# One gate tile of each of the first three attention rounds moved into the last round of a hybrid decoder layer

## What is computed

```python
n = rmsnorm(h) ; proj = n @ w_in         # q_A k_A v_A q_B k_B v_B (512 each) gate_A gate_B (1024 each)
o_a = dilated_attention(rope(q_a), rope(k_a), v_a)      # 8 heads of 64
o_b = stick_breaking_attention(q_b, k_b, v_b)           # 8 heads of 64
mixed = sigmoid(gate_a) * (o_a @ w_up_a) + sigmoid(gate_b) * (o_b @ w_up_b)
h = h + mixed @ w_out
h = h + memory_attention(rmsnorm(h), rmsnorm(mem))
h = h + swiglu(rmsnorm(h)) ; return rmsnorm(h)
```

## Time and profile before

| | us |
|---|---|
| median of 3 runs (lowest, highest) | 1866.86 (1864.33, 1867.20) |
| the profiled execution's own time | 1866.63 |
| its span, first to last instruction | 1864.8 |
| PE busy | 1733.5 (93% of the span) |
| DVE busy | 1143.5 (61%) |
| ACT busy | 777.6 (42%) |
| POOL busy | 766.9 (41%) |
| start of the four rounds on PE | 121.09, 299.10, 476.35, 653.69 |
| start of the gated stage on PE | 818.35 |

### The profile page before, as it was taken

The page is one execution under the profiler, slowest core; times in us unless marked ns, Lnnn a source line. Parts: engine busy times, 40 slices in busy tenths (PEclk is TensorE's granted clock), DMA queues, the critical chain, the costliest instruction groups (busy, mean ns, idle before and its releaser), DMA issues.

```text
span 1864.8 us, 24982 instructions
## 1 busy us (share of the span) xinstructions
PE 1733.5 (93%) x8346; PEld 1401.5 (75%) x8346; DVE 1143.5 (61%) x1688; ACT 777.6 (42%) x1283; POOL 766.9 (41%) x892
## 2 busy tenths in 40 slices
PE   3799999999999999969999887999999999999996
PEld 3677777777777777758887765788888888788884
DVE  6446795689468856965444568645545455566666
ACT  4214773577358647852222344433433334110012
POOL 5732222332223221224454112665666656533445
PEclk8899999999999999979999888999999999999998
DMA  5311112111211211164212000122121221332222
GB/s 185 134 40 43 42 50 66 46 29 57 69 36 39 67 51 40 50 245 147 102 45 91 23 12 22 46 104 76 67 90 67 97 83 67 139 108 92 90 90 91
DMA packets 51711, 141.73 MB, mean 76 GB/s; under 512 B 6192, under 2 KB 14640, under 8 KB 51504
## 3 DMA queue, kind: packets, MB, share of 16 engines
q1 hardware_dynamic: 30816, 98.73, 15.0%
q10 hardware_dynamic: 20816, 41.95, 6.8%
HBM read 109.20 MB, written 30.41 MB: 75 GB/s over the span
## 4 chain that ended last, share of the span: by engine, by line
PE 79%; DVE 6%; issue 5%; ACT 3%; POOL 2%; ACTq 0%; DMA 0%; DVEq 0%; POOLq 0%
PE ps L492 45%; PE ps L811 22%; PE ps L638 4%; PE ps L601 3%; PE ps L615 3%; POOL w_lo L461 1%; DVE e_row L1530 1%; POOL rms L473 1%; DVE pt L1560 1%; DVE e_row L1527 1%; DVE h L1889 1%; DVE rows L1539 1%; PE ps L634 1%; POOL w_lo L446 0%; ACT p_m L1173 0%
## 5 line engine op out<-in xcount | busy, mean ns | idle before, releaser
L441 POOL TENSOR_SCALAR w_hi<-w_stage 128x512 fp32r<-128x512 f32 x188 | 128.3, 700 | 884.5 <-issue 457.9
L446 POOL TENSOR_TENSOR w_lo<-w_stage,w_hi 128x256 fp32r<-128x256 f32 x376 | 346.7, 952 | 7.9
L492 PE MATMUL ps<-n_hi,w_hi 128*128 128x512 f32 x1184 | 329.9, 400 | 14.2 <-DVE n_lo L1480 7.1
L492 PE MATMUL ps<-n_lo,w_hi 128*128 128x512 f32 x1184 | 321.8, 393 | 0.0
L492 PE MATMUL ps<-n_hi,w_lo 128*128 128x512 f32 x1184 | 321.2, 392 | 0.0
L492 PEld LDWEIGHTS ps<-n_hi,w_hi 128*128 128x128 f32 x1184 | 222.1, 191 | 62.7 <-issue 16.5
L492 PEld LDWEIGHTS ps<-n_lo,w_hi 128*128 128x128 f32 x1184 | 221.9, 189 | 46.0 <-issue 0.2
L492 PEld LDWEIGHTS ps<-n_hi,w_lo 128*128 128x128 f32 x1184 | 220.2, 188 | 44.9
L461 POOL TENSOR_TENSOR w_lo<-w_stage,w_hi 128x256 fp32r<-128x256 f32 x176 | 163.7, 950 | 146.9 <-ACT w_hi L1207 146.9
L1630 DVE TENSOR_TENSOR h<-ps,h 128x512 f32<-128x512 f32 (+1 forms) x176 | 121.3, 690 | 127.2 <-PE ps L492 127.2
L1029 ACT ACTIVATE pt<-ps 128x256 fp32r<-128x256 f32 (+3 forms) x96 | 78.0, 812 | 134.9 <-PE ps L615 134.9
(11 more groups left out here) (224 smaller groups left out, 2997.2 us busy)
## 6 DMA issues: line engine op xcount, KB each, us to landing
w_stage<-weights_in SPq DMA_DIRECT2D x116, 512.0 KB, 3.4
w_stage<-weights_in SPq DMA_DIRECT2D x44, 256.0 KB, 2.7
hidden_scratch<-u_f SPq DMA_DIRECT2D x22, 512.0 KB, 5.7
n_lo<-hidden_scratch SPq DMA_DIRECT2D x22, 512.0 KB, 4.0
gates_scratch<-raw ACTq DMA_DIRECT2D x16, 512.0 KB, 2.8
o_scratch<-o_sum ACTq DMA_DIRECT2D x64, 64.0 KB, 2.1
n_lo<-o_scratch ACTq DMA_DIRECT2D x8, 512.0 KB, 4.1
g_a<-gates_scratch ACTq DMA_DIRECT2D x8, 512.0 KB, 3.7
```

What stands on the lines that cost most here:

```text
L441: ins = pool.tensor_scalar(w_hi[:, b, at], stage[:, b, at], 1.0, 1.0, ALU.mult, ALU.mult)
L446: ins = pool.tensor_tensor(w_lo[:, b, at], stage[:, b, at], w_hi[:, b, at].bitcast(F32), ALU.subtract)
L492: ins = pe.matmul(bank, w[:, b, c:c + P], mv(k), start=(first and n == 0), stop=(last and n == total - 1))
```

## The change

The first three rounds get three gate tiles instead of four, and the last round seven instead of four, 9, 9, 9 and 10 tiles in place of 10, 10, 10 and 7. In the first three rounds the value tile of B now stands ahead of the query and key tile of A, and one pass is gone from each of slots 0 to 5. The last round has passes in all its 28 slots. The rounds are written out (Python loops in place of `Fori`), so that all semaphore counts and addresses in them are constants. `LOAD_O` and `ROUND_O` are gone: all eight output tiles are loaded, rounded and split behind the last pass of the last round (ACT waits for `bank_full` of `B_GATED`). The total number of passes is the same (222).

```diff
-TILES_IN = 10
+TILES_IN = 9
+GATES_IN = 3
-ROUND = Plan(("KB", "QB", "QA", "KA", "VB", "VA", "G0", "G1", "G2", "G3"),
-             [3] * 6 + [2] * 6 + [3, 2, 3, 2, 3, 2, 2, 3, 2] + [1] * 6 + [2], {"TB": (12, 14), "TA": (18, 20)})
-LAST = Plan(("KB", "QB", "VB", "G0", "G1", "G2", "G3"),
-            [2] * 21 + [0] * 7, {"TB": (10, 12)})
-LOAD_O = {max(LAST.end.values()) + 2 + n: [k for k in (2 * n, 2 * n + 1) if k < KT - 1] for n in range(4)}
-ROUND_O = {min(LOAD_O) + 3 + k: k for k in range(4)}
+ROUND = Plan(("KB", "QB", "VB", "QA", "KA", "VA", "G0", "G1", "G2"),
+             [2] * 12 + [3, 2, 3, 2, 3, 2, 2, 3, 2] + [1] * 6 + [2], {"TB": (10, 12), "TA": (18, 20)})
+LAST = Plan(("KB", "QB", "VB", *[f"G{n}" for n in range(2 * KT - GATES_IN * (PAIRS - 1))]),
+            [2] * 12 + [3, 2, 3, 2, 3, 2, 2, 3, 2] + [2] * 7, {"TB": (10, 12)})
+def stores(i, m):
+    before = sum(n % 2 == m % 2 for n in range(GATES_IN)) * i
+    return 1 + before + m // 2
...
-            with pe.Fori(0, PAIRS - 1) as i:
+            for i in range(PAIRS - 1):
                 round_(i, ROUND)
             round_(PAIRS - 1, LAST)
...
                         elif what == "store":
                             m = int(name[1])
                             act.wait_ge(bank_free, bank + (unit + 2))
-                            act.dma_start(gates_d[bass.ds(i * 4 + m, 1), :, :].rearrange("o p n -> p (o n)"),
+                            act.dma_start(gates_d[i * GATES_IN + m],
                                           raw[:, RAW[name], :]).then_inc(gate_out[m % 2], 16)
...
-                    if plan is LAST and s in LOAD_O:
-                        act.wait_ge(bank_full, B_GATED)
-                        for b in range(2):
-                            act.wait_ge(o_out[b], 16 + 16 * (QUERIES // 2 * i + QUERIES // 4))
-                        for k in LOAD_O[s]:
-                            act.dma_start(n_lo[:, k, :].bitcast(F32), o_d[k]).then_inc(tile_in[k], 16)
-                    if plan is LAST and s in ROUND_O:
-                        round_o(ROUND_O[s])
...
             for b in range(2):
                 act.wait_ge(o_out[b], PAIRS * QUERIES // 2 * 16 + 16)
+            act.wait_ge(bank_full, B_GATED)
+            for k in range(KT):
+                act.dma_start(n_lo[:, k, :].bitcast(F32), o_d[k]).then_inc(tile_in[k], 16)
             for b in range(2):
-                act.wait_ge(gate_out[b], PAIRS * 2 * 16 + 16)
-            act.dma_start(n_lo[:, KT - 1, :].bitcast(F32), o_d[KT - 1]).then_inc(tile_in[KT - 1], 16)
+                act.wait_ge(gate_out[b], 16 * stores(PAIRS - 1, len(LAST.names) - 3 + (len(LAST.names) - 3 + b) % 2))
             load_gates(0, 0)
             load_gates(1, 1)
-            for k in range(len(ROUND_O), KT):
+            for k in range(KT):
                 round_o(k)
...
-                    if plan is LAST and s - 1 in ROUND_O:
-                        o_rest(ROUND_O[s - 1])
...
-            for k in range(SLOTS + 1 - min(ROUND_O), KT):
+            for k in range(KT):
                 o_rest(k)
```

More of the change, by code:

```diff
@@ L40 @@
 NEG_MAX = -3.0e38
-TILES_IN = 10
-N_TILES = PAIRS * TILES_IN + KT + KT + MH + 2 * MH + KT // 2 + 6 * FPAIRS
+TILES_IN = 9
+GATES_IN = 3
+N_TILES = 5 * KT + KT + KT + MH + 2 * MH + KT // 2 + 6 * FPAIRS
 G_MIX, G_MEMQ, G_MEMKV, G_FFN, G_FINAL = (KT * n for n in range(5))
@@ L150, in __init__ @@
             work.sort(key=lambda w: w[0] == "rope")
-ROUND = Plan(("KB", "QB", "QA", "KA", "VB", "VA", "G0", "G1", "G2", "G3"),
-             [3] * 6 + [2] * 6 + [3, 2, 3, 2, 3, 2, 2, 3, 2] + [1] * 6 + [2], {"TB": (12, 14), "TA": (18, 20)})
-LAST = Plan(("KB", "QB", "VB", "G0", "G1", "G2", "G3"),
-            [2] * 21 + [0] * 7, {"TB": (10, 12)})
-LOAD_O = {max(LAST.end.values()) + 2 + n: [k for k in (2 * n, 2 * n + 1) if k < KT - 1] for n in range(4)}
-ROUND_O = {min(LOAD_O) + 3 + k: k for k in range(4)}
-RAW = {"QA": 0, "KA": 1, "VA": 2, "KB": 0, "QB": 1, "VB": 2, "G0": 0, "G1": 1, "G2": 0, "G3": 1}
+ROUND = Plan(("KB", "QB", "VB", "QA", "KA", "VA", "G0", "G1", "G2"),
+             [2] * 12 + [3, 2, 3, 2, 3, 2, 2, 3, 2] + [1] * 6 + [2], {"TB": (10, 12), "TA": (18, 20)})
+LAST = Plan(("KB", "QB", "VB", *[f"G{n}" for n in range(2 * KT - GATES_IN * (PAIRS - 1))]),
+            [2] * 12 + [3, 2, 3, 2, 3, 2, 2, 3, 2] + [2] * 7, {"TB": (10, 12)})
+RAW = {"QA": 0, "KA": 1, "VA": 2, "KB": 0, "QB": 1, "VB": 2, **{f"G{n}": n % 2 for n in range(KT)}}
 SPLIT_NUMBER = {"KB": 3, "QB": 4, "QA": 5, "KA": 6, "TB": 3, "TA": 5}
 HEAD_TILES = 3
+def stores(i, m):
+    before = sum(n % 2 == m % 2 for n in range(GATES_IN)) * i
+    return 1 + before + m // 2
 HEAD_UNITS = 2 * HEAD_TILES
@@ L336, in build @@
         W_MIX = 2 * MH
-        W_GATED = W_MIX + PAIRS * TILES_IN
+        W_GATED = W_MIX + 5 * KT
         W_OUT = W_GATED + KT
@@ L661, in round_ @@
                             tile = W_MIX + HEAD_TILES + plan.tile[name]
-                            unit_pass(i * TILES_IN + (tile + 1), tile % 2, half, p, bank + (unit - 1))
+                            unit_pass(i * TILES_IN + (tile + 1), (i * TILES_IN + tile) % 2, half, p, bank + (unit - 1))
             for tile in range(3):
@@ L1091, in _ @@
             act.activation(zero_r[:], ident[:], ACT.Copy, scale=0.0).then_inc(mask_ready, 1)
-            with act.Fori(0, PAIRS - 1) as i:
+            for i in range(PAIRS - 1):
                 round_(i, ROUND)
@@ L1545, in round_ @@
                                  "G1": 6 if plan is ROUND else 4}.get(name)
-                        stored = {"KB": 1, "QB": 1, "G2": 2, "G3": 2}.get(name)
+                        stored = None
+                        if name in ("KB", "QB"):
+                            stored = stores(i, RAW[name])
+                        elif name[0] == "G" and int(name[1]) >= 2:
+                            stored = stores(i, int(name[1]))
                         if half == 0 and split:
@@ L1549, in round_ @@
                         if half == 0 and stored:
-                            dve.wait_ge(gate_out[RAW[name]], i * 32 + 16 * stored)
+                            dve.wait_ge(gate_out[RAW[name]], 16 * stored)
                         read_out(name, half, bank + (unit))
@@ L1589, in _ @@
             dve.wait_ge(bias_in, 32)
-            with dve.Fori(0, PAIRS - 1) as i:
+            for i in range(PAIRS - 1):
                 round_(i, ROUND, LINKS)
@@ L1919, in weight_stream @@
             if n[0] == "G":
-                out.append(w[24 + 4 * i + int(n[1])])
+                out.append(w[24 + GATES_IN * i + int(n[1])])
             else:
```

## The result

The changed kernel takes 1876.50 us (median of 5 runs, 1874.33 to 1878.59), the kernel before 1864.33 (5 runs, 1861.20 to 1867.20). The ratio is 1.0061, 95% interval 1.0050 to 1.0072: slower by 12.2 us, where I had forecast 3.7. It is inside the range of 8 in 10 (1856 to 1880) and just above the range of the forecast case (1866 to 1876).

A forecast was written before the change was run, and what follows sets the result against it. PE, busy 93% of the span, was taken as the bound, with DVE nearly full in the B half. Three rounds -17.7 us, last round and reload +21.4: +3.7 on 1866.63, so 1870.3 us; 8 in 10 range 1856 to 1880.

The forecast's parts named there:

- forecast case: Whole kernel: -17.7 us from three rounds, +21.4 from last round and reload, 1870.3 us, range 1866 to 1876, chance 0.50.
- The A half: Slots 0 to 11 of rounds one to three: only PE bounds them, so all 11.0 us of six passes come off.
- The ropes: B half, rounds one to three: two ropes moved there on DVE bring back 5.1 us a round, bounds 1.8 and 8.3.
- the clock: B half: TensorE's clock may fall behind a longer PE wait, 0.3 us a round, bounds 0 and 1.6.
- the work on DVE: DVE, slots 14 to 23: +5.45 us a round from moved ropes and low parts, -0.6 from waits on constants.
- The rule on POOL and DVE: Ropes in the B half: sharing the SBUF interface, a rope meeting POOL's split would take longer than 3.63 us.
- The low part of `KA` in DVE's wait: Slot 19: 1.21 us more on DVE falls into its 1.62 us wait for ACT and costs nothing.
- Rival 1: B half: ropes hidden by the lag between PE and DVE, 1860.4 us or, with nothing, 1855.0, faster; chance 0.18.
- Rival 2: B half: ropes cost all they can, 8.3 us a round, PE waits dropping the clock, 1879.9 us, slower; chance 0.16.
- Rival 3: Behind the last round: shorter exposed reload, PE starting some 10 us behind the last pass, 1864.8 us; chance 0.08.
- Rival 4: Loop's branch: if PE stood there too, two branches back give 2 x 2.6 us, 1865.2, no change; chance 0.05.
- The last round and the reload: Last round's start to a warm gated stage: 189.1 us against 167.7 before, +21.4, bounds 16 and 26.

The follow-up runs named there:

- narrow ropes: Changed kernel with the three DVE operations of each rope in the rounds cut from 1024 to 128 columns: 1854.38 us, ratio 0.9941.
- light split: Changed kernel with POOL forming only one quarter of the low part of each weight tile of the rounds: 1866.79 us, ratio 1.0004.
- one rope early: Changed kernel with `QA` ahead of `VB`, its rope back in the A half: 1858.69 us; with the reload's first reordering 1864.89, with its second 1854.09.

## Why the prediction was right or wrong

- **The stage was right, the direction a narrow call.** The point was 1870.3 us (+3.7 against the profiled execution of before), measured 1876.5 (+9.9). Slower had the largest chance, 0.41, but no change had 0.37, and +3.7 stood on the border between them. The range held the time; the size was off by more than half.
- **The A half: right.** Slots 0 to 11 take 66.24 us as forecast, 10.4 below 76.65. Another 0.4 of PE's work went from slot 14 (9.77 instead of 10.18 us), which has one V transposition fewer. With narrow ropes the whole round is 10.9 us shorter (166.37), of which 0.5 is what writing out gives.
- **The ropes: the mechanism was right, the term was too small.** I put 5.1 us a round, bounds 1.8 and 8.3; it measured 11.0 - 3.2 = 7.8, and the kernel with narrow ropes gives 7.65 in round two and 7.2 over three. Three rounds give -9.75 us in place of -17.7. The step that failed is the sum of what comes back on DVE, in two of its parts. First, the clock: I took 0.3 us, because a wait of 2.72 us had cost nothing before. The wait of slot 19 became 3.41 us and cost 2.5 us of slow matmuls (PE busy 70.82 instead of 68.29 us). Second, the work on DVE: I had 5.45 - 0.6 = 4.85 us, and DVE came out 6.4 later and PE's waits 6.1 longer. "The sum above goes by the row" took 3.63 us for each rope from rows in the A half, where POOL's split didn't stand beside them; the first rope took 5.0, and with the split cut down slot 15 was 1.35 us shorter. With these two, 5.1 - 0.3 + 2.5 + 1.35 = 8.65, and slots 12 to 20 measured 77.8 - 69.2 = 8.6. That this agrees to the last digit is luck: a pair of scans that ran 2.23 us beside the first split before runs 1.81 now, a copy beside the second takes 0.53 instead of 0.17, and such terms, which I left out, cancel.
- **The end of the round.** The round is -10.4 + 8.6 - 1.4 = -3.2: slots 21 to 27 got 1.4 shorter. Their waits are as long as before (3.3 and 3.2 us), but PE is busy 26.66 instead of 28.17 us and the granted clock is 1.00 instead of 0.95. I had no such term; why the clock stays up there now is open.
- **The rule on POOL and DVE was the better guide than my row.** On the rule of the Trainium skill, GPSIMD Engine Reference, Specifications, that the two share their SBUF interface, the trace agrees: 1.63 to 1.75 us beside a split against 1.21 apart from it, and the experiment with a light split shows the split as the cause. It doesn't slow every such operation: in the kernel before, the low part of `QA` at 402.37 took 1.21 us inside the split of 400.02. I had named the rule and left it out of the sum.
- **The low part of `KA` in DVE's wait: right.** That wait shrank from 1.62 to 0.89 us. The wait of a pass for its read-out behind the rope (1.49 us, slot 15) was missing from my list; I had counted read-outs and not asked who waits for them.
- **Rival 1** (hidden ropes) fell: 7.65 us. **Rival 2** is the one that the runs fit best. Its mechanism was waits on PE that drop the clock, and its sign a granted clock well under 0.9 in slots 16 and 19: slot 19 has 0.76, slot 16 only waits. In size it was nearer than my forecast too, 7.8 against 8.3 a round and 9.9 of 13.3 in all. **Rival 3** fell: 16.7 us. **Rival 4**: writing the loop out gives 3.2 us in all, so it is worth more than nothing. In the trace 0.7 of it lie in an earlier start and 2.2 in the three rounds (530.4 instead of 532.6 us). That is some 0.7 a round, about the 0.6 that I had put down for constants in DVE's waits, but slots 12 to 20, where I had put it, show only 0.2 of it. PE has no wait at the branch in either kernel.
- **The last round and the reload: right**, 189.1 us as forecast, +21.4. Of its parts the round was 1.3 shorter and the wait 1.2 longer than I had put. That they cancel is luck.

## What to carry to other kernels

Before moving a tile, ask of both engines that share a stage: most of the work taken from PE in the stage that PE bounds came back in the stage that DVE bounds, through two ropes of three vector operations each that had been free where they stood. When the forecast of a stage hangs on a queue that is 94% busy, price added work with the durations seen beside its new neighbours, and count the clock behind each wait that grows. Small stores that others wait for go ahead of large loads in the issue order, and waits for them behind all work that doesn't need them.

## What the runs showed of the hardware that I had not expected

- Two waits of PE of the same length, 2.13 and 2.12 us, in the same slot of two rounds of one execution: the clock stayed at 1.00 behind the one and was 0.85 over the slot behind the other, 10.15 against 11.76 us. It is so in the kernels with one rope early too: slot 19 waits 1.74 to 1.77 us in all nine traced rounds, and takes 9.8 us in six and 11.3 to 11.4 in three. The length of such a wait alone doesn't give its price; what else decides it no run shows.
- The three DVE operations of a rope, each on two SBUF tensors of 128x1024, took 1.63 to 1.75 us beside POOL's split, 1.21 to 1.23 apart from it. The size varies: in the kernel before, the same kind of operation (L1444) took 1.21, 1.29 and 1.44 us inside three splits. A pair of scans of 128x256 took 2.20 us beside a split and 1.28 apart from one. The split took 5.76 us beside the rope and 2.82 to 3.81 in the A half: both sides pay.
- A store of 64 KB issued behind 3.5 MB of loads on ACT's queue landed after 10.7 us, ahead of them after 2.6.
